# DeltaNet core of a four-layer trunk: query-key products move to the crossing bank and are scaled behind the last step, lower-block products are issued per head into the next decay bank

## What is computed

```python
def chunk_gated_delta(q, k, v, g, beta, s0):
    g = jnp.cumsum(g.reshape(b, h, n, c), axis=-1)
    decay = jnp.where(incl, jnp.exp(jnp.where(incl, diff, 0.0)), 0.0)
    kb = k * beta[..., None]
    a = jnp.where(strict, jnp.einsum('bhnid,bhnjd->bhnij', kb, k) * decay, 0.0)
    lower = a + jnp.eye(c, dtype=a.dtype)
    sol = lax.linalg.triangular_solve(lower, rhs, left_side=True, lower=True, unit_diagonal=True)
    qk = jnp.einsum('bhnid,bhnjd->bhnij', q, k) * decay
    def step(s, xs):
        v_new = u_c - jnp.einsum('bhck,bhkv->bhcv', w_c, s)
        o_c = (jnp.einsum('bhck,bhkv->bhcv', q_c * jnp.exp(g_c)[..., None], s)
               + jnp.einsum('bhij,bhjv->bhiv', qk_c, v_new))
```

## Time and profile before

| what | us |
|---|---|
| median of three runs | 2249.74 |
| the profiled execution | 2248.5 |
| its span, first to last instruction | 2246.7 |
| DeltaNet core of layer 0, from the first `s_gc` to the last output copy | 191.75 to 312.56 |
| DeltaNet core of layer 3, the same | 1674.47 to 1796.34 |

### The profile page before, as it was taken

One profiled execution on the slowest core, in us unless ns is written; L12 is line 12 of the kernel. 1 busy time (PEld: TensorE's weight loads), 2 busy tenths in 40 slices (PEclk: granted clock), 3 DMA queues, 4 the chain that ended last, 5 costly groups with the idle time before them and its releaser, 6 DMA issues.

```text
span 2246.7 us, 44490 instructions
## 1 busy us (share of the span) xinstructions
PE 2152.6 (96%) x19589; PEld 1623.2 (72%) x19589; DVE 764.7 (34%) x1704; ACT 380.3 (17%) x794; POOL 127.3 (6%) x221
## 2 busy tenths in 40 slices
PE   6998889999999999999999999999988899999998
PEld 4776778888888645646687788888877776556465
DVE  2235644777323200000312354562346532000002
ACT  1124341000101000000222210002143330000001
POOL 4000011111000000000100011010000000000000
PEclk8999999999999999999999999999999999999999
DMA  9963039987455699999755798653430077999992
GB/s 341 272 243 114 13 124 343 333 288 259 137 191 186 231 388 382 380 381 380 263 159 192 257 346 284 207 181 110 150 131 8 14 255 254 387 381 379 383 383 99
DMA packets 363977, 550.94 MB, mean 245 GB/s; under 512 B 12176, under 2 KB 312080, under 8 KB 358464
## 3 DMA queue, kind: packets, MB, share of 16 engines
q1 hardware_dynamic: 336288, 466.59, 60.3%
q0 software_dynamic: 21968, 76.84, 10.4%
q10 hardware_dynamic: 5536, 4.73, 0.6%
HBM read 537.64 MB, written 14.93 MB: 246 GB/s over the span
## 4 chain that ended last, share of the span: by engine, by line
PE 77%; SPq 11%; DVE 5%; DMA 4%; ACT 2%; issue 2%; ACTq 0%; DVEq 0%
PE ps L681 74%; SPq L506 7%; SPq L510 3%; DMA work<-in_ada_w 2%; DMA ring<-in_moe_w_down 1%; ACT ring L1543 1%; DVE ring L2108 1%; DVE work L1966 1%; DVE ring L2148 1%; ACT work L1543 1%; PE ps L867 0%; DMA ring<-in_ada_w 0%; PE ps L1232 0%; DVE hT L1976 0%; DVE work L2550 0%
## 5 line engine op out<-in xcount | busy, mean ns | idle before, releaser
L681 PE MATMUL ps<-hT,ring 128*128 128x256 f32 x3200 | 713.2, 382 | 2.9 <-DVE hT L1976 2.5
L681 PE MATMUL ps<-ring,work 128*32 128x384 f32 (+7 forms) x8008 | 694.5, 438 | 16.0 <-DMA ring<-in_moe_w_gu 5.3
L681 PEld LDWEIGHTS ps<-hT,ring 128*128 128x128 f32 x3200 | 608.1, 191 | 114.9 <-issue 21.4
L681 PEld LDWEIGHTS ps<-ring,work 128*32 128x32 f32 (+2 forms) x8008 | 391.1, 115 | 297.3 <-issue 179.1
L1543 ACT ACTIVATE work<-ps 128x256 f32<-128x256 f32 (+6 forms) x220 | 100.7, 468 | 1327.8 <-PE ps L681 1146.8
L681 PE MATMUL ps<-work,ring 128*128 128x256 f32 (+1 forms) x1344 | 283.6, 369 | 0.2 <-DVE work L2533 0.2
L681 PEld LDWEIGHTS ps<-work,ring 128*128 128x128 f32 (+1 forms) x1344 | 238.3, 185 | 33.8 <-issue 1.1
L2550 DVE SCALAR_TENSOR_TENSOR work<-work,csil 128x1024 f32<-128x1024 f32 x196 | 239.5, 1279 | 40.5 <-DMA work<-in_ada_w 40.1
L681 PE MATMUL ps<-ring 64*64 64x64 f32 (+1 forms) x4192 | 158.1, 237 | 26.3 <-ACT ring L1543 12.3
L681 PEld LDWEIGHTS ps<-ring 64*64 64x64 f32 x4192 | 133.5, 141 | 44.2 <-ACT ring L1543 20.3
L1543 ACT ACTIVATE ring<-ps 128x384 f32<-128x384 f32 (+4 forms) x208 | 91.5, 443 | 296.5 <-PE ps L681 286.7
(11 more groups left out here) (268 smaller groups left out, 1102.1 us busy)
## 6 DMA issues: line engine op xcount, KB each, us to landing
ring<-in_moe_w_gu SPq DMA_DIRECT2D x96, 1536.0 KB, 16.0
ring<-in_moe_w_down SPq DMA_DIRECT2D x48, 1536.0 KB, 16.5
work<-in_ada_w POOLq DMA_DIRECT2D x112, 512.0 KB, 6.5
ring<-in_ff_w_gu SPq DMA_DIRECT2D x88, 512.0 KB, 7.7
ring<-in_ada_w SPq DMA_DIRECT2D x40, 1024.0 KB, 8.0
ring<-in_dn_w_in SPq DMA_DIRECT2D x32, 1024.0 KB, 5.6
ring<-in_moe_w_gu SPq DMA_DIRECT2D x32, 1024.0 KB, 8.9
ring<-in_ff_w_down SPq DMA_DIRECT2D x44, 512.0 KB, 9.1
```

What stands on the lines that cost most here:

```text
L681: return pe.matmul(out, lhsT, rhs, start=start, stop=stop, **kw)
```

## The change

- `s_kk` makes only the key-key products. The query-key products become a step of their own, `s_kq`, for each head, ahead of that head's `s_t`; they go to columns 256 to 511 of the crossing bank, which the other steps don't use.
- On DVE the product `QD` leaves `s_qd` and becomes `s_q`, run for both heads behind the last level (after the last `s_crossed`), with a semaphore `d_q` of its own. `s_qd` now ends with the addition, which raises `d_qd`.
- ZB goes. `s_z` runs for each head: it waits for the ACT copy of its own head, and writes columns 0 to 255 of the decay bank X of the next pair. On ACT `s_z` waits for its own head's products and for `d_q`.
- The order on PE in a middle round is now: `s_z` of head 0, `s_kq` and `s_t` of head 0, `s_z` of head 1, `s_tz` of head 0, `s_kq` and `s_t` of head 1, `s_tz` of head 1.

```diff
--- before.py
+++ after.py
@@ -298,7 +298,7 @@
...
-        d_dec, d_qd, d_m, d_r0, d_v, d_t = (sem("d_" + n) for n in ("dec", "qd", "m", "r0", "v", "t"))
+        d_dec, d_qd, d_m, d_r0, d_v, d_t, d_q = (sem("d_" + n) for n in ("dec", "qd", "m", "r0", "v", "t", "q"))
...
@@ -322,7 +322,7 @@
...
-        PAIRS, ZB = H // 2, 4
+        PAIRS = H // 2
...
@@ -871,10 +871,15 @@
                     if h >= 2:
                         pe.wait_ge(a_ut, nth(hd - 2, LEV - 1, LEV))
                     for g in range(2):
-                        q, kk = qT[:, h, g * P:(g + 1) * P], kT[:, h, g * P:(g + 1) * P]
-                        mm(cols(Y, g), kk, kk)
-                        ins = mm(cols(Y, 2 + g), kk, q)
+                        kk = kT[:, h, g * P:(g + 1) * P]
+                        ins = mm(cols(Y, g), kk, kk)
                     ins.then_inc(p_kk, 1)
+
+                def s_kq(h, w, hd, X, Y):
+                    if hd >= 2:
+                        pe.wait_ge(d_q, hd - 1)
+                    for g in range(2):
+                        mm(cols(crossing(h % 2), 2 + g), kT[:, h, g * P:(g + 1) * P], qT[:, h, g * P:(g + 1) * P])
                 def s_ks(j):
                     if j == 0 or l == 0:
@@ -974,16 +979,14 @@
                 lo, hi = slice(0, HB), slice(HB, P)
                 half = [(0, lo, hi), (2, hi, lo), (1, lo, hi), (3, hi, lo)]
-                def s_z(j):
-                    last = head(l, j, 1)[2] + 1
-                    if l == 0:
-                        pe.wait_ge(d_ar, ada_turned[0])
-                    pe.wait_ge(a_y, last)
-                    for p in range(2):
-                        w = head(l, j, p)[1]
-                        for c, src, dst in half:
-                            ins = mm(ps[dst, ZB, (2 * p + c % 2) * P:(2 * p + c % 2 + 1) * P], AT(l, w)[src, c, dst],
-                                     MM(l, w)[src, c, :])
+                def s_z(j, p):
+                    _, w, hd, _, _ = head(l, j, p)
+                    free = head(l, j + 1, p)[3]
+                    if j == PAIRS - 1:
+                        pe.wait_ge(a_o, hd - 1)
+                    pe.wait_ge(a_y, hd + 1)
+                    for c, src, dst in half:
+                        ins = mm(ps[dst, free, (c % 2) * P:(c % 2 + 1) * P], AT(l, w)[src, c, dst], MM(l, w)[src, c, :])
                     ins.then_inc(p_z, 1)
                 def s_tz(h, w, hd, X, Y):
@@ -1017,14 +1020,18 @@
                         s_ks(j)
                     if old:
                         both(s_y, j - 1)
-                        s_z(j - 1)
+                        s_z(j - 1, 0)
                     if new:
+                        s_kq(*head(l, j, 0))
                         s_t(*head(l, j, 0))
                     if old:
-                        both(s_tz, j - 1)
+                        s_z(j - 1, 1)
+                        s_tz(*head(l, j - 1, 0))
                     if new:
+                        s_kq(*head(l, j, 1))
                         s_t(*head(l, j, 1))
                     if old:
+                        s_tz(*head(l, j - 1, 1))
                         both(s_o, j - 1)
                     for lev in range(1, LEV if new else 1):
                         both(s_w(lev), j)
@@ -1648,10 +1655,11 @@
                     f(flat(MM(l, w)), ps[:, X, :], ACT.Copy).then_inc(a_y, 1)
                 def s_z(h, w, hd, X, Y):
-                    p = h % 2
-                    act.wait_ge(p_z, hd // 2 + 1)
-                    f(TT(l, w)[HB:P, 0:2, :], ps4(ZB)[HB:P, 2 * p:2 * p + 2, :], ACT.Copy, scale=-1.0)
-                    f(TT(l, w)[0:HB, 2:4, :], ps4(ZB)[0:HB, 2 * p:2 * p + 2, :], ACT.Copy, scale=-1.0) \
+                    free = head(l, h // 2 + 1, h % 2)[3]
+                    act.wait_ge(d_q, hd + 1)
+                    act.wait_ge(p_z, hd + 1)
+                    f(TT(l, w)[HB:P, 0:2, :], ps4(free)[HB:P, 0:2, :], ACT.Copy, scale=-1.0)
+                    f(TT(l, w)[0:HB, 2:4, :], ps4(free)[0:HB, 0:2, :], ACT.Copy, scale=-1.0) \
                         .then_inc(a_z, 1)
                 def s_o(h, w, hd, X, Y):
@@ -2133,9 +2141,13 @@
                             ins = tt(MW(l, w)[to, 2 * d:2 * d + 2], AT(l, w)[r, 2 * d:2 * d + 2, r],
                                      level(0)[r, d], ALU.mult)
                     link(ins)
-                    tt(UT(l, w)[:, 1], MW(l, w), identc[:, None, :].to_broadcast([P, 4, HB]), ALU.add)
-                    tt(four(QD(l, w)), ps4(Y)[:, None, 2:4, :].to_broadcast([P, 2, 2, P]), four(TT(l, w)),
-                       ALU.mult).then_inc(d_qd, 1)
+                    tt(UT(l, w)[:, 1], MW(l, w), identc[:, None, :].to_broadcast([P, 4, HB]), ALU.add) \
+                        .then_inc(d_qd, 1)
+
+                def s_q(h, w, hd, X, Y):
+                    dve.wait_ge(p_ut, nth(hd, LEV - 1, LEV))
+                    tt(four(QD(l, w)), ps4(crossing(h % 2))[:, None, 2:4, :].to_broadcast([P, 2, 2, P]),
+                       four(TT(l, w)), ALU.mult).then_inc(d_q, 1)
                 def s_qe(h, w, hd, X, Y):
                     dve.wait_ge(a_qe, hd + 1)
@@ -2182,7 +2194,9 @@
                     for lev in range(1, LEV if j < PAIRS else 1):
                         both(s_m(lev), j)
                         both(s_crossed(lev), j)
-                        if lev < LEV - 1 and j + 1 < PAIRS:
+                        if lev == LEV - 1:
+                            both(s_q, j)
+                        elif j + 1 < PAIRS:
                             s_dec((lev - 1) % 2)(*head(l, j + 1, (lev - 1) // 2))
                 for m in range(4):
```

## The result

| | before | after |
|---|---|---|
| median, comparison on record | 2250.2 us (4 runs) | 2236.76 us (4 runs, 2236.14 to 2242.93) |
| ratio, 95% interval | | 0.9945 [0.9931, 0.996] |
| median, second comparison (run r1 below) | 2251.7 us (16 runs) | 2237.18 us (5 runs, 2232.31 to 2240.14) |
| ratio, 95% interval | | 0.9929 [0.9915, 0.9942] |
| profiled execution, span | 2248.5, 2246.7 | 2242.93, 2241.1 |

By the ratios the change takes 12 to 16 us, 0.55 to 0.71%, off the time; by the medians 13.4 and 14.5 us. The forecast was 10.9 us and 2238.8 us, with a range from 2233.5 to 2242.5. The profiled execution of the changed kernel is the slowest of the first four; its rows are read for the cores and not for the whole.

What follows compares the result with a forecast made beforehand. PE, busy in 96% of the span, was taken to set the time; 6 x 1.0 + 2 x 1.2 + 2 x 1.25 = 10.9 us off the 2249.74 us median gave 2238.8 us, range 2233.5 to 2242.5.

Steps and rivals of the forecast that it cites:

- Middle rounds: Rounds 1 to 3 of two layers: the first `s_w` comes 1.0 us earlier in each of six.
- both waits on ACT: Middle round: PE's waits for ACT's copy of head 1 and four small copies vanish, other PE work lying in them.
- PE's time up to head 1's `s_t`: Middle round: PE's steps added end to end, asking for head 1's factors at 254.71, DVE ready at 254.57.
- Rival (2): Middle rounds: DVE becomes the bound, gain falls to about 0.5 us each, 2241.8 us in all; chance 0.12.
- DVE's margin: Middle round: DVE raises `d_qd` ahead of PE's asking by 0.49 us for head 0, 0.14 for head 1.
- The changes of shape: Middle round: four more tiling-mode changes on PE; `s_kq` takes 0.58 us instead of 0.46.
- Rival (3): Six middle rounds: 24 more shape changes at 0.7 us each make the kernel slower, about 2254 us; chance 0.02.
- Round 0: First round of each layer: both heads' `s_qd` products leave the path PE waits on, 1.2 us per layer.
- rival (1): Round 0: PE's clock stays up, 2 to 3 us more per layer, 2236.3 or 2233.8 us; chance 0.22.
- Round 4: Round with only the old pair: `s_z`, small copies and `s_tz` of head 0 start earlier, 1.25 us per layer.
- What comes behind the cores: Loads and all later stages start earlier by what the core saves; nothing at a fixed time takes it back.
- Rival (4): Middle rounds: head 0's copies come no earlier, about 0.5 us of each left; counted in Rival (2)'s 0.12.

Runs made afterwards that it cites:

- r1: The changed kernel run once more, with no edit: 2237.18 us, ratio 0.9929.
- r2: The query-key part of the change alone; the lower-block products stay one step for both heads behind ACT's second copy: 2243.52 us, ratio 0.9967.
- r6: The changed kernel with DVE's query-key scaling cut to 8 columns of each block, outputs made from the key-key factors: 2237.54 us.
- r5: The changed kernel with the scaling of the query-key products done twice on DVE for each head: 2244.66 us.
- r7: r6 with the order of r4, both edits on the changed kernel: 2235.35 us.
- r4: The changed kernel with both heads' query-key products right behind the products with the state, adding no change of shape: 2239.01 us, ratio 0.9938.
- r9: The changed kernel with one more 128x512 product on DVE, for the first pair alone, ahead of the release of the transposes: 2240.86 us, ratio 0.9956.
- r10: The changed kernel with products into an unused bank in PE's waits of round 0, also ahead of the first level: 2236.25 us, ratio 0.9933.
- r3: The lower-block part of the change alone, per head; query-key products and their scaling put back where they were: 2246.71 us, ratio 0.9976.
- r8: The changed kernel with round 0's query-key products also issued ahead of the state products and three times per head: 2238.9 us, ratio 0.9951.

## Why the prediction was right

**The time and the sign** came out: the measured 2236.76 is 2.0 us under the forecast. That the number lies so near is in part luck: the gain was larger, 13.4 and 14.5 us by the medians and 15.8 and 13.7 in the cores against 10.9, and the forecast's start, 2249.74, lay under the medians measured beside the change. By stages, in the two profiles of the changed kernel:

- *Middle rounds:* forecast 1.0 us each, measured 1.25 in layer 0 and 1.17 in layer 3, so some 7.3 instead of 6.0 in the six. The 0.08 between the layers is the dropped wait on `d_ar` (r2), which the prediction left out. The mechanism, that both waits on ACT close because other work of PE lies in them, is what the chain shows. The mis-sized term is PE's time up to head 1's `s_t`: I added up `s_z`, `s_t` and `s_tz` end to end, and reckoned that PE would ask for it at 254.71 and DVE be ready at 254.57. From one `s_kq` to the other my sum has 2.38 us (251.75 to 254.13), the timeline after 1.95 (249.13 to 251.08). On the same count (2.64 us later than the profile after) DVE was ready at 254.46 and PE was there before it; taking DVE away brings 0.14 us (r6).
- *Rival (2), the wait on DVE,* is therefore there, in every middle round, but not at the price that I gave it: it did not take back half of the gain. It took 0.14 us of a gain that was larger than forecast. That DVE's margin was next to nothing was right, and r5 shows what it means: from here on a product added on DVE is paid in full.
- *The changes of shape:* forecast 0.12 us for each `s_kq` from the earlier trace rows, measured 0.08 (r7). Rival (3) is out by a factor of more than ten. The rule of the Trainium skill (TensorEngine Tiling (Array Packing), Key Properties), that a change of tiling mode drains TensorE, fits r7 in sign (0.16 us for four changes). In the changed kernel the price is hidden behind the wait on DVE (r4), so it decided nothing.
- *Round 0:* forecast 1.2 us per layer, measured 1.1 and 2.2 in r1, 2.9 and 3.6 in the profile on record. The 1.2 is DVE's shorter `s_qd`: r9, which makes that list long again, is 1.1 longer in layer 0 than r1, where the clock is low for as long. The rest is rival (1), the clock. It came in part, which I had not put as a case: up all through round 0 in one execution, low for a shorter stretch in the other. Against r10, where the clock stays up, r9 is 3.0 us longer per layer, so by this some 1.8 of them are the clock.
- *Round 4:* from the table, round 3 and 4 less a middle round, 8.5 us in layer 0 before, 7.7 in the profile on record and 7.5 in r1; so 0.7 and 1.0 of the forecast 1.25, and 1.25 exactly from ACT's copy to `s_o`. Most of what is missing in the first is PE's unexplained wait shown above. In layer 3 it is 9.1 before, 7.8 and 7.0 after, so 1.3 and 2.1, of which 1.17 from ACT's copy to `s_o`; there the profile before has such unexplained waits of PE.
- *What comes behind the cores:* that it takes nothing back fits the medians to some 2 us (13.4 and 14.5 against 15.8 and 13.7 in the cores) and is not shown closer than that; both profiled executions lost 10.2 and 5.3 us outside the cores against the one before.
- *Rival (4)* is out: head 0's copy comes before head 1's products end.

That the low clock of round 0 comes from PE's idle time there is supported and not shown. For it speaks the count: with DVE's list long (before, r3, r9) the clock fell in all six round 0s, with it short and `s_kq` elsewhere (r4, r7) in all four, with it short and `s_kq` in PE's waits (after, r1, r2, r5, r6) in five of ten, and with most of those waits filled (r10) in neither of two. Against it stand r8, where the same waits went with a fall in one layer and none in the other, and that r10 is one execution: both layers stayed up in the profile on record and in r2 too, without any filling. Which execution of the changed kernel has the fall and which not was not settled. By the Trainium skill (TensorE: Matmul & The Clock Gate, What's actually happening) activity releases the throttle; the count agrees as far as it goes. Not tried: a shorter list on DVE in the middle rounds with the right result. r7, which leaves nearly all of the scaling out and has r4's order, bounds both together at 0.3 us per round, 1.8 us in all.

## What to carry to other kernels

Where two chains end within a few tenths of a us of each other, shortening one alone gives little or nothing, and the two changes together give much more than their sum: read the second-latest arrival of a wait before pricing an edit. Work that is needed late (here the query-key products and their scaling) belongs out of a chain that is waited for early, and into an idle stretch of its engine. Compare stages between profiles, not only whole times; here the whole times would have told a story in which the parts add up.

## What the runs showed of the hardware

The granted clock of TensorE fell in round 0 though PE never stood idle for more than 1.73 us at a time there (r9). The same waits of 1.00 and 0.45 us went with a fall in layer 3 and with none in layer 0 of one execution (r8); with most of them filled it stayed up in both layers of the one execution seen (r10). With the same program one execution had it low and another not, worth 1.8 and 1.4 us in the two layers (25.99 and 25.53 against 24.23 and 24.13).

Four more changes between 128x128 and 64x64 products cost PE 0.16 us in a stretch that it runs without a break, 0.04 us each (r6 and r7). A second semaphore to wait for ahead of a step of PE came with 0.14 us from the release to the step, one alone with 0.04 (before, layers 0 and 3).

The middle round of the changed kernel, at full clock, took 26.43 us in both layers of both executions.
